# Two blocks on one Trainium2 core: the matmuls of the second block's attention stage issued as pairs of column halves, its transposes left full width

## The reference, cut to what matters

```python
kv = rmsnorm(kv_lat, kv_norm)                       # one latent key/value of width 128 per token
logits = einsum('bqhc,bqkc->bhqk', q_b, kv_sel) * scale + bias   # 16 heads, admitted keys only
probs = softmax(where(valid, logits, -inf))
o = einsum('bhqk,bqkc->bqhc', probs, kv_sel)
...
xbc = conv(proj[xbc columns]) ; xs, Bm, Cm = split(silu(xbc))    # 4096 columns of h @ w_in
```

## Time and profile before

| what | value |
|---|---|
| median of 3 runs | 1309.13 us (1308.36 to 1311.02) |
| the profiled execution's own time | 1308.58 us |
| its span, first to last instruction | 1306.6 us |
| outside the span | 1.98 us |
| TensorE busy | 1293.0 us, 99% of the span |
| VectorE, ScalarE, GpSimd busy | 941.5, 426.4, 185.2 us |
| mean granted clock of TensorE | 0.998 of 2.4 GHz |

### The profile page before, as it was taken

The page is one execution under the profiler, slowest core; times in us unless marked ns, Lnnn a source line. Parts: engine busy times, 40 slices in busy tenths (PEclk is TensorE's granted clock), DMA queues, the critical chain, the costliest instruction groups (busy, mean ns, idle before and its releaser), DMA issues.

```text
span 1306.6 us, 32615 instructions
## 1 busy us (share of the span) xinstructions
PE 1293.0 (99%) x14429; PEld 1153.6 (88%) x14429; DVE 941.5 (72%) x1602; ACT 426.4 (33%) x929; POOL 185.2 (14%) x164
## 2 busy tenths in 40 slices
PE   8999999999999999999999999999999999999998
PEld 7975899988898589998877899999999986999986
DVE  3985798556688479857881799788888845866753
ACT  2254334220226433332055424455742103100101
POOL 3100422030000042204134000003200100011100
PEclk9999999999999999999999999999999999999999
DMA  9632567576433257767638895137645554645540
GB/s 326 202 130 97 194 239 278 206 267 238 163 129 129 97 195 260 260 223 268 216 98 241 220 248 150 60 121 253 208 134 186 175 192 130 194 151 176 179 178 32
DMA packets 132923, 243.06 MB, mean 186 GB/s; under 512 B 7237, under 2 KB 37725, under 8 KB 132273
## 3 DMA queue, kind: packets, MB, share of 16 engines
q1 hardware_dynamic: 122506, 218.00, 48.7%
q0 software_dynamic: 9872, 22.80, 7.4%
q10 hardware_dynamic: 407, 0.20, 0.1%
HBM read 231.49 MB, written 6.34 MB: 182 GB/s over the span
## 4 chain that ended last, share of the span: by engine, by line
PE 91%; DVE 5%; DMA 1%; ACT 1%; POOL 1%; issue 1%; SPq 0%; DVEq 0%
PE acc L2192 56%; PE scr L2192 17%; PE pvw L2192 9%; DVE mid L1512 2%; PE ptb L2306 1%; PE scr L2804 1%; PE pvw L2811 1%; DMA ring<-in_w_mem_kv 1%; PE scr L2297 1%; PE ptb L2192 1%; PE pvw L2316 1%; PE ptb L2636 0%; DMA strip_rows<-hid 0%; DVE hid L1860 0%; PE pvw L2322 0%
## 5 line engine op out<-in xcount | busy, mean ns | idle before, releaser
L2192 PE MATMUL acc<-y,ring 128*64 128x128 f32 (+3 forms) x1760 | 154.5, 285 | 0.0
L2192 PEld LDWEIGHTS acc<-y,ring 128*64 128x64 f32 (+2 forms) x1760 | 141.8, 152 | 7.7 <-ACT y L959 1.2
L2192 PE MATMUL acc<-ring,big 128*128 128x256 f32 (+1 forms) x376 | 115.6, 453 | 0.0
L2192 PEld LDWEIGHTS acc<-ring,big 128*128 128x128 f32 x376 | 70.6, 190 | 33.4 <-issue 27.0
L2192 PE MATMUL acc<-ring,hid 128*128 128x256 f32 (+1 forms) x364 | 99.1, 417 | 0.0
L2192 PE MATMUL acc<-x,ring 128*64 128x128 f32 (+1 forms) x1472 | 98.9, 278 | 0.0
L2192 PEld LDWEIGHTS acc<-x,ring 128*64 128x64 f32 (+1 forms) x1472 | 89.6, 139 | 4.7 <-issue 3.2
L895 ACT ACTIVATE ring<-ring,silc 128x512 f32<-128x512 f32 x96 | 60.1, 709 | 95.2 <-DMA ring<-in_ada_w 95.1
L2192 PEld LDWEIGHTS acc<-ring,hid 128*128 128x128 f32 x364 | 68.4, 190 | 22.2 <-issue 14.9
L2192 PE MATMUL acc<-ysq,ring 128*64 128x128 f32 x1248 | 75.0, 273 | 0.1
L2192 PEld LDWEIGHTS acc<-ysq,ring 128*64 128x64 f32 x1248 | 69.8, 137 | 0.4 <-ACT ysq L1076 0.4
(11 more groups left out here) (581 smaller groups left out, 2767.5 us busy)
## 6 DMA issues: line engine op xcount, KB each, us to landing
ring<-in_w_in SPq DMA_DIRECT2D x24, 2048.0 KB, 11.4
ring<-in_w_up SPq DMA_DIRECT2D x16, 2048.0 KB, 8.5
ring<-in_w_down SPq DMA_DIRECT2D x16, 2048.0 KB, 8.0
ring<-in_ada_w SPq DMA_DIRECT2D x12, 2048.0 KB, 13.4
ring<-in_w_ffn_in SPq DMA_DIRECT2D x22, 1024.0 KB, 6.9
ring<-in_w_out SPq DMA_DIRECT2D x6, 2048.0 KB, 8.2
ring<-in_w_o_ssd SPq DMA_DIRECT2D x4, 2048.0 KB, 9.1
ring<-in_w_ffn_out SPq DMA_DIRECT2D x4, 2048.0 KB, 7.8
```

Source lines behind the costliest of these rows:

```text
L2192: ins = pe.matmul(dst, w, m, start=start, stop=stop, is_transpose=turned, skip_group_check=True)
```

## The change

`half_product` (336 matmuls in the stage), `scores2` (32) and `values2` (32) call `column_halves` in place of `mm` and `pe.matmul`. The transposes are as before. The work computed is the same, and no wait, buffer or order changes.

```diff
@@ scores2
                 for m in range(2):
-                    ins = pe.matmul(scr[i % 2][:, m, :], q2[:, 2 * j + m, t * P:(t + 1) * P], kvn[:, :], start=True, stop=True)
+                    ins = column_halves(scr[i % 2][:, m, :], q2[:, 2 * j + m, t * P:(t + 1) * P], kvn[:, :], True, True)
                 ins.then_inc(s_full, 1)
@@ values2
                 for kt in range(TT):
-                    ins = pe.matmul(pvb[:, 0:2, :], kvtok[:, kt, :], pt[:, i % 2, kt:kt + 3:2, :], start=kt == 0, stop=kt == 1)
+                    ins = column_halves(pvb[:, 0:2, :], kvtok[:, kt, :], pt[:, i % 2, kt:kt + 3:2, :], kt == 0, kt == 1)
                 ins.then_inc(o_full, 1)
@@ half_product
                 for k in range(4):
-                    ins = mm(dst[:, i * P:(i + 1) * P], w[:, k, i * P:(i + 1) * P], a[:, k, :], opens and i == 0 and k == 0, k == 3)
+                    ins = column_halves(dst[:, i * P:(i + 1) * P], w[:, k, i * P:(i + 1) * P], a[:, k, :], opens and i == 0 and k == 0, k == 3)
                 return ins
```

## The result

| | before | after |
|---|---|---|
| median | 1309.2 us (7 runs, 1308.36 to 1311.02) | 1313.18 us (7 runs, 1312.92 to 1314.39) |
| profiled execution | 1308.58 us, span 1306.6 | 1312.97 us, span 1310.9 |
| ratio | | 1.0032, 95% interval 1.0022 to 1.0041 |

The change made the kernel slower, by 4.0 us where 3.1 were forecast. The page after has 1600 records more, and TensorE is still busy for 99% of the span.

The account below looks back on a forecast made before the run. The prediction took TensorE's own work, busy 1293.0 of 1306.6 us, to bound the kernel. Its terms, -1.7 + 0 + 4.8 + 0 + 0 = +3.1 us, gave 1311.9 us, range 1309.8 to 1313.9 (its own narrower range 1310.8 to 1313.2).

Parts of the forecast that it names:

- The stage is TensorE's own pace: Changed stage, 761 to 871 us: it has no TensorE waits and is as long as TensorE's own work.
- Terms 1 to 4: Stage: products gain 1.68 us, scores and values 0, shape changes around 16 transposes groups lose 4.8, borders cancel to 0.
- term 1: The stage's 42 products: each gains 0.040 us in halves, 1.68 us in all.
- Term 3: Shape changes around the stage's 16 transposes groups: 0.30 us a group, about 0.15 each change, 4.8 us lost.
- Term 5: What hangs on the change: some 1600 more records to fetch, earlier ring slot release, possible new waits; 0 us.
- The delay reaches the end: After the stage: the whole delay moves as one piece past VectorE's line 1900, whose stall stays 1.0 us.
- rival 2: The later stall on line 1900 gives back 1.0 us: +2.1, 1310.7 to 1311.2 us; 10%.
- Rival 1: The stage's changes of shape are hidden, leaving only the products' gain of 1.7 us: 1306.9 us; 4%.
- Rival 3: New stalls around the slots, from VectorE's load or waits inside halves: one or two make +4.5, 1313.5 us; 6%.

Follow-up runs that it names:

- plain_halves: The changed kernel with its transposes issued as ordinary matmuls with the identity, in halves too: 1315.41 us, ratio 1.0046.
- attention_only: The kernel before with only scores and values (`scores2`, `values2`) in halves, products full width: 1319.26 us, ratio 1.0075.
- products_only: The kernel before with only the 336 matmuls of `half_product` in halves, scores and values full width: 1315.03 us, ratio 1.0045.
- before_pool_late: The kernel before, with GpSimd's first-block feed-forward products waiting until VectorE has finished four weight sums: 1308.37 us, ratio 0.9995.
- after_pool_late: The changed kernel, with GpSimd's first-block feed-forward products waiting until VectorE has finished four weight sums: 1311.64 us, ratio 1.0018.
- squares_halves: The kernel before, with only the two full-width matmuls of `mean_squares2`, at 1042.58 us, in halves: 1308.07 us, ratio 0.9991.

## Why the prediction was right, and what it missed

The result lies in the range and on the side forecast, and the steps can be checked one by one. The time itself, 1313.18 us, is 1.3 us above the 1311.9 that the prediction names and at the very end of its narrower range, 1310.8 to 1313.2. About 0.4 us of this is the choice of a start between the profiled execution and the median; 0.9 us were lost outside the stage, where the sum has no term. That even the narrower range holds the result is luck; the growth of the stage is not.

- *The stage is TensorE's own pace:* right. No wait in it before or after.
- *Terms 1 to 4:* right. The sum was +3.1 us; the stretch between the marker groups grew by 3.13. `plain_halves`, which has the gain of term 1, no change of shape and 16 times 0.44 us more, came out at 5.28 for 5.3, so the gain and the cost are right each by itself and not only in their difference.
- *Term 3 had about 0.15 us for each change.* On going from halves to transposes and back that holds. Back to full matmuls it is 0.20 us (`attention_only`, `products_only`), which the prediction did not need.
- *Term 5, no new waits and nothing from the longer program:* right in the stage. The semaphores are reached late enough, and VectorE's 19.7 us of 20 did no harm.
- *The delay reaches the end:* right. The stall on line 1900 is still 1.0 us, 52 us after the stage, as the chain had it; rival 2 falls. TensorE is 4.54 us late behind the stage and still 4.36 where the kernel before is at 1233 us.
- *Rival 1* (changes of shape hidden) falls with every run. *Rival 3* came out at its size of some 4.5 us in part, 4.0, but not by its mechanism: nothing stalled in the stage.
- *What was missed:* 0.9 us outside the stage. The prediction took the other 1170 us of the kernel as fixed. They hold a near tie in each layer of the first block, worth 1.0 us, that a transfer's landing some 0.5 us sooner or later decides. The kernel before lost it in neither layer in one profile and in one layer in the other; the changed kernel lost it in both layers in both profiles. Since no instruction ahead of the ties differs between the programs, the profiles say how the 0.9 us are lost, and `before_pool_late` and `after_pool_late` show that most of them go with the tie. Why the transfer takes longer with the changed program is open. `products_only` and `plain_halves`, the other two long programs, lost both ties, `attention_only` one and `squares_halves` none, which fits a dependence on the length of the program, but no run changed the length alone. If it is the length, the part of the sum that failed is the 0 that term 5 has for the 1600 records more.

## What to carry to other kernels

Before giving a matmul another tile shape, count how often TensorE will go from one shape to the other, and read the price of one such change from a place in the trace that has it: here 0.15 to 0.20 us, as much as 4 to 5 of the 40 ns that a whole product gains in halves. A half-done change of shape can be worse than either end, as `attention_only` and `products_only` are, and a lone full-width group between halves (or the reverse) is worth looking for by itself. When two profiles differ ahead of the place that was changed, look for two engines that start within the spread of a transfer of one another; a wait that settles their order can gain more than the change did.

## What the runs showed of the hardware

- For float32 with 128 moving columns a product of 8 matmuls takes 1.787 us full width and 1.747 in halves; with 256 columns the two are equal (0.86 us for two matmuls). What halves gain thus depends on the moving columns: 0.04 us in 1.79 with 128 of them, and nothing that the rows resolve with 256.
- A change of shape has two parts: about 0.10 us at the border, and 0.05 us (halves, transposes) to 0.10 us (full matmuls) more between the first records of the new shape. In `after` the second transpose of a group starts 0.17 us after the first, at a pace of 0.11; in `attention_only` the second record of a full product starts 0.21 us after the first, at the same pace.
- A change of the kind of work, or a semaphore already reached, costs nothing that the rows show as long as the shape stays (0.87, 0.87 and 0.86 us in `plain_halves`).
- A VectorE sum of two tensors of 128 x 1024 takes 1.22 us alone and 3.37 us beside a GpSimd product of the same size; which of them starts first, by 0.02 us in the closest case and 0.75 in the widest, decided 1.0 us of the kernel's time.
